# One MoE decoder layer pair on one core: experts ranked by load on the chip, two of the eight turns with two 32-slot tiles

## The reference, cut to what matters

```python
def moe_swiglu(x, w_router, w_gu, w_down):
    b, s, d = x.shape
    xt = x.reshape(b * s, d)                       # 256 tokens x 1024
    logits = (xt @ w_router).astype(jnp.float32)   # 8 experts
    top_vals, top_idx = lax.top_k(logits, TOP_K)   # TOP_K = 2
    gates = jax.nn.softmax(top_vals, axis=-1)
    combine = jnp.sum(jax.nn.one_hot(top_idx, N_EXPERTS, dtype=jnp.float32) * gates[..., None], axis=1)
    y = jnp.zeros((b * s, d), jnp.float32)
    for e in range(N_EXPERTS):
        gu = xt @ w_gu[e]                          # 1024 x 5632, gate and up
        g, u = gu[..., :D_FF_EXPERT], gu[..., D_FF_EXPERT:]
        y = y + combine[:, e:e + 1] * ((jax.nn.silu(g) * u) @ w_down[e])   # 2816 x 1024
    return y.astype(x.dtype).reshape(b, s, d)
```

## Time and profile before

| | us |
|---|---|
| median of 3 runs | 1282.19 (1281.58 to 1284.21) |
| the profiled execution, its own time | 1283.65 |
| its span | 1281.9 |
| TensorE busy | 1226.9 (96%) |
| VectorE / ScalarE busy | 297.0 / 213.8 |
| granted TensorE clock, mean | 0.98 |

### The profile page before, as it was taken

One profiled execution on the slowest core, in us unless ns is written; L12 is line 12 of the kernel. 1 busy time (PEld: TensorE's weight loads), 2 busy tenths in 40 slices (PEclk: granted clock), 3 DMA queues, 4 the chain that ended last, 5 costly groups with the idle time before them and its releaser, 6 DMA issues.

```text
span 1281.9 us, 23541 instructions
## 1 busy us (share of the span) xinstructions
PE 1226.9 (96%) x10557; PEld 656.7 (51%) x10558; DVE 297.0 (23%) x509; ACT 213.8 (17%) x336; POOL 8.1 (1%) x40
## 2 busy tenths in 40 slices
PE   7878999999998889999999999999999999999988
PEld 5548999985884443533533533533533533533433
DVE  4754545533235310001001001001001001001021
ACT  3353443432134100000000000000000000000020
POOL 2000000000000000000000000000000000000000
PEclk9888999999999879999999999999999999999999
DMA  9706655540322346999999999999999999998330
GB/s 333 252 12 216 200 181 184 195 165 33 132 106 92 124 172 251 408 409 405 408 408 384 353 355 375 353 355 371 358 350 375 357 351 373 359 360 331 125 140 33
DMA packets 114170, 344.23 MB, mean 269 GB/s; under 512 B 7773, under 2 KB 30874, under 8 KB 114074
## 3 DMA queue, kind: packets, MB, share of 16 engines
q1 hardware_dynamic: 114074, 342.74, 71.7%
HBM read 341.67 MB, written 1.05 MB: 267 GB/s over the span
## 4 chain that ended last, share of the span: by engine, by line
PE 93%; DVE 4%; ACT 1%; issue 1%; DMA 0%; DVEq 0%; ACTq 0%
PE ps L1624 37%; PE ps L1675 12%; PE ps L1680 6%; PE ps L1385 5%; PE ps L1401 5%; PE ps L1402 5%; PE ps L1403 5%; PE ps L1605 3%; PE ps L1521 2%; PE ps L1774 2%; PE ps L1648 1%; PE ps L1461 1%; PE ps L1693 1%; PE ps L1251 1%; PE ps L1276 1%; PE ps L1298 1%
## 5 line engine op out<-in xcount | busy, mean ns | idle before, releaser
L1624 PE MATMUL ps<-wring,xg 128*32 128x512 f32 (+1 forms) x5376 | 479.6, 503 | 2.8 <-DVE e_h L1152 2.0
L1624 PEld LDWEIGHTS ps<-wring,xg 128*32 128x32 f32 x5376 | 181.1, 110 | 281.7 <-issue 229.5
L1675 PE MATMUL ps<-wring,ehT 128*32 128x512 f32 x1408 | 169.1, 593 | 0.6 <-ACT ehT L737 0.6
L1401 PE MATMUL ps<-dn_high,w_high 128*128 128x256 f32 x352 | 100.6, 286 | 2.5 <-DVE dn_low L1029 2.5
L1402 PE MATMUL ps<-dn_low,w_high 128*128 128x256 f32 x352 | 100.5, 286 | 0.0
L1403 PE MATMUL ps<-dn_high,w_low 128*128 128x256 f32 x352 | 100.4, 285 | 0.0
L1675 PEld LDWEIGHTS ps<-wring,ehT 128*32 128x32 f32 x1408 | 45.2, 110 | 97.4 <-issue 95.9
L1680 PE MATMUL ps<-wring,ehT 128*32 128x512 f32 x704 | 93.2, 592 | 0.0
L1020 DVE TENSOR_TENSOR w_low<-ring,w_high 128x2048 fp32r<-128x2048 f32 x33 | 75.6, 2292 | 58.5 <-ACT w_high L637 58.5
L737 ACT COPY ehT<-ps 128x384 f32<-128x384 f32 x24 | 11.5, 481 | 432.3 <-PE ps L1648 248.8
L1162 DVE COPY ehT<-ps 128x384 f32<-128x384 f32 (+1 forms) x24 | 11.8, 491 | 305.7 <-PE ps L1648 185.6
(11 more groups left out here) (245 smaller groups left out, 962.2 us busy)
## 6 DMA issues: line engine op xcount, KB each, us to landing
wring<-in_w_exp_gu SPq DMA_DIRECT2D x128, 1024.0 KB, 7.7
wring<-in_w_exp_down SPq DMA_DIRECT2D x88, 1024.0 KB, 7.3
wring<-in_w_exp_gu SPq DMA_DIRECT2D x64, 768.0 KB, 8.6
ring<-in_w_ffn_gu SPq DMA_DIRECT2D x44, 512.0 KB, 5.4
ring<-in_w_ffn_down SPq DMA_DIRECT2D x11, 1024.0 KB, 4.9
ring<-in_w_ple_gate SPq DMA_DIRECT2D x4, 1024.0 KB, 4.9
ring<-in_w_q_b SPq DMA_DIRECT2D x4, 1024.0 KB, 4.9
ring<-in_w_o_b SPq DMA_DIRECT2D x4, 1024.0 KB, 6.4
```

Of the source, the lines that this page charges most:

```text
L1401: pe.matmul(out, high_l, high_r, start=first, stop=False)
L1624: return pe.matmul(ps[32 * quarter:32 * quarter + 32, bank, c0:c0 + 2 * nf * P], xg[:, k, 32 * b:32 * b + 32], w[:, :, f * P:(f + nf) * P] ...
L1675: pe.matmul(ps[32 * q:32 * q + 32, 3, :], turned(g, 2 * u + r, b), w[:, r, half * 512:(half + 1) * 512], start=(g == 0 and u == 0 and r == ...
```

## The change

A constant table gives each of the eight turns a number of tiles: turns 3 and 7 have two, the others three. Turn 0 is always expert 0. The other experts are ranked by load on VectorE (`order_experts`), and `TURN_RANK` says which rank comes at which turn: the two smallest loads of experts 1 to 7 come at turns 3 and 7. `expert_at` holds the expert of each turn; SyncE reads it into a register at each turn for the addresses of the loads. Gates and slots are put into the order of the turns (`turn_gate`, `turn_slot`). All steps of an expert take the number of tiles as an argument; for two tiles `gate_up` has 8 (group 2: 12) matmuls in a unit instead of 12 (18), `down` 8 instead of 12, the scatter one part instead of two. The loops of SyncE, ScalarE and VectorE become unrolled. The overflow branch is taken when any turn's load is above its own capacity (96 or 64), and runs two three-tile passes for each such turn. In `first_groups` the transposes of the selection matrix move ahead of group 1. `k_squares` shares its SBUF place with another early tile.

```diff
-NB = SLOTS // 32
+TILES = (3, 3, 3, 2, 3, 3, 3, 2)
+TURN_RANK = (0, 1, 2, 6, 3, 4, 5, 7)
+PINNED = 1024.0
...
     @block.sync
-        loads("body", BODY, 0, lambda i: 1 if BODY[i][0] == "gu" and BODY[i][1] < 2 else 0, "first")
-        with sp_.Fori(1, E - 1) as e:
-            nxt = sp_.snap(e + 1)
-            loads("body", BODY, e, lambda i: nxt if BODY[i][0] == "gu" and BODY[i][1] < 2 else e, "body")
-        loads("alone", ALONE, E - 1, lambda i: E - 1, "end")
-        sp_.wait_ge(route_done, 1)
+        e = 0
+        for n in range(E - 1):
+            if n == 0:
+                sp_.wait_ge(order_done, 1)
+            after = sp_.value_load(expert_at[0:1, n + 1:n + 2], min_val=0, max_val=E - 1)
+            loads("body", BODY, n, lambda i: after if BODY[i][0] == "gu" and BODY[i][1] < 2 else e, "body" if n else "first")
+            e = after
+        loads("alone", ALONE, E - 1, lambda i: e, "end")
...
-        largest = sp_.value_load(counts[0:1, E:E + 1], min_val=0, max_val=T)
-        with sp_.If(largest > SLOTS):
+        largest = sp_.value_load(excess[0:1, E:E + 1], min_val=0, max_val=T)
+        with sp_.If(largest > 0):
...
     @block.gpsimd
         link(pool.tensor_copy(slot_no[:], slot_no_i[:]))
+        link(pool.memset(turn_cap[:], float(SLOTS)))
+        for i in range(E):
+            link(pool.memset(turn_rank[:, i:i + 1], float(TURN_RANK[i])))
+            if i == 0 or TILES[i] < 3:
+                link(pool.memset(turn_cap[:, i:i + 1], 32.0 * TILES[i] + (0.0 if i else PINNED)))
...
     @block.scalar
+        def silu(g, n, kind, nb):
 
             used(kind, "gu", g, n - 1 if kind == "body" and g < 2 else n)
             if g < 2:
-                act.activation(e_silu[:].rearrange("p (b c) n -> p b (c n)", b=NB), ps[:, 0:NB, 0:256], ACT.Silu).then_inc(e_silu_done, 1)
+                act.activation(e_silu[:, 0:2 * nb].rearrange("p (b c) n -> p b (c n)", b=nb), ps[:, 0:nb, 0:256], ACT.Silu).then_inc(e_silu_done, 1)
...
+        def result_high(n, kind, nb):
             used(kind, "down", 2, n)
-            for part in range(2):
-                act.copy(ye_high[:, part, :], ps[:, 3 + part, :]).then_inc(e_y_high, 1)
+            for part in range(nb - 1):
+                act.copy(ye_high[:, part, :], ps[:, 3 + part, :]).then_inc(e_y_high, 4 - nb)
...
     @block.vector
         dve.wait_ge(pos_ready, 1)
-        link(dve.memset(slot_of[:], 0.0))
...
-        dve.tensor_reduce(counts[:, E:], ps[:, 2, 0:E], AX.X, ALU.max)
-        dve.tensor_copy(counts[:, 0:E], ps[:, 2, 0:E]).then_inc(route_done, 1)
+        dve.tensor_copy(load[:], ps[:, 2, 0:E]).then_inc(route_done, 1)
+
+        def order_experts():
+
+            dve.wait_ge(route_done, 1)
+            link(dve.tensor_scalar(load[:, 0:1], load[:, 0:1], PINNED, None, ALU.add))
+            other, own = bc(load[:].unsqueeze(1), [P, E, E]), bc(load[:].unsqueeze(2), [P, E, E])
+            dve.tensor_tensor(cmp_gt[:, 0], other, own, ALU.is_gt)
+            link(dve.tensor_tensor(cmp_eq[:, 0], other, own, ALU.is_equal))
+            link(dve.tensor_tensor(cmp_eq[:, 0], cmp_eq[:, 0], earlier[:], ALU.mult))
+            link(dve.tensor_tensor(cmp_gt[:, 0], cmp_gt[:, 0], cmp_eq[:, 0], ALU.add))
+            link(dve.tensor_reduce(load_rank[:], cmp_gt[:, 0], AX.X, ALU.add))
+            link(dve.tensor_tensor(hot[:], bc(load_rank[:].unsqueeze(1), [P, E, E]), bc(turn_rank[:].unsqueeze(2), [P, E, E]), ALU.is_equal))
+            dve.tensor_tensor(cmp_gt[:, 0], hot[:], bc(slot_no[:, 0, 0:E].unsqueeze(1), [P, E, E]), ALU.mult)
+            link(dve.tensor_tensor(cmp_gt[:, 1], hot[:], bc(load[:].unsqueeze(1), [P, E, E]), ALU.mult))
+            dve.tensor_reduce(turn_no[:], cmp_gt[:, 0], AX.X, ALU.add)
+            link(dve.tensor_reduce(turn_load[:], cmp_gt[:, 1], AX.X, ALU.add))
+            link(dve.tensor_tensor(turn_load[:], turn_load[:], turn_cap[:], ALU.subtract))
+            link(dve.tensor_scalar(turn_load[:], turn_load[:], 0.0, None, ALU.max))
+            dve.tensor_copy(expert_at[:], turn_no[:])
+            dve.tensor_reduce(excess[:, E:], turn_load[:], AX.X, ALU.max)
+            dve.tensor_copy(excess[:, 0:E], turn_load[:]).then_inc(order_done, 1)
+            for src, dst in ((gate, turn_gate), (slot_of, turn_slot)):
+                link(dve.tensor_tensor(hot_of[:], bc(hot[:].unsqueeze(1), [P, NT, E, E]), bc(src[:].unsqueeze(2), [P, NT, E, E]), ALU.mult))
+                link(dve.tensor_reduce(dst[:], hot_of[:], AX.X, ALU.add))
...
+        def picks(slots, base, k, nb):
...
+            c = (nb - 1) * P
             for t in range(NT):
-                ins = dve.tensor_scalar(pick[:, t, :], slot_no[:, base, :], slot_of[:, t, bass.ds(e, 1)], None, ALU.is_equal)
+                ins = dve.tensor_scalar(pick[:, t, 0:c], slot_no[:, base, 0:c], slots(t), None, ALU.is_equal)
             ins.then_inc(e_pick, 1)
...
+        picks(lambda t: slot_of[:, t, 0:1], 0, 0, TILES[0])
+        for half in range(2):
+            gathered(0, half, TILES[0])
+        order_experts()
+        product(0, 0, TILES[0])
+        turned_high(0, 0, TILES[0])
+        turn_picks(1)
+        product(1, 0, TILES[0])
+        for n in range(E - 1):
+            both_experts(n)
...
     @block.tensor
+            m = 32 * nb
             for c in range(4 * half, 4 * half + 4):
                 for t in range(NT):
-                    ins = pe.matmul(ps[:, 7, (c % 4) * SLOTS:(c % 4 + 1) * SLOTS], hs[:, t, c * P:(c + 1) * P], pick[:, t, 64:64 + SLOTS],
+                    ins = pe.matmul(ps[:, 7, (c % 4) * m:(c % 4 + 1) * m], hs[:, t, c * P:(c + 1) * P], pick[:, t, 64:64 + m],
                                     start=(t == 0), stop=(t == NT - 1))
...
                 if g < 2:
-                    for b in range(NB):
+                    for b in range(nb):
                         for j in range(4):
                             ins = part(j, b, 2 * j, 2, b, 0, first)
                 else:
-                    for b in range(NB):
+                    for b in range(nb):
                         for j in range(4):
                             part(j, b, j, 1, b, 0, first)
-                    for b in range(NB):
+                    for b in range(nb):
                         for j in range(2):
                             ins = part((2 * b + j) % 4, b, 4 + j, 1, b // 2, 256, False)
...
-            for i in range(6 if g < 2 else 4):
-                ins = pe.transpose(ps[:, 5 + i // 3, (i % 3) * P:(i % 3 + 1) * P], e_h[:, i, :], ident[:])
-            if g == 2:
+            for i in range(2 * nb if g < 2 else nb + 1):
+                ins = pe.transpose(ps[:, 5 + i // nb, (i % nb) * P:(i % nb + 1) * P], e_h[:, i, :], ident[:])
+            if g == 2 and nb == 3:
...
-                for half in range(2):
+                for half in range(2 if nb == 3 else 0):
                     for r in range(2):
                         q = 2 * half + r
...
             for t in range(NT):
-                for part in range(2):
+                for part in range(nb - 1):
                     for ye in (ye_high, ye_low):
...
-        def first_groups(n, spare=0):
+        def first_groups(n, nb):
 
             for half in range(2):
-                gather(n, half, spare)
-            gate_up("lead", 0, n)
-            gate_up("lead", 1, n, range(0, 4))
-            turn(0, n)
-            turn_pick(n)
-            gate_up("lead", 1, n, range(4, KD))
+                gather(n, half, nb)
+            gate_up("lead", 0, n, nb)
+            turn_pick(n, nb)
+            gate_up("lead", 1, n, nb, range(0, 4))
+            turn(0, n, nb)
+            gate_up("lead", 1, n, nb, range(4, KD))
...
-        first_groups(0)
+        first_groups(0, TILES[0])
         for e in range(E - 1):
             both_experts(e)
-        last_groups(E - 1)
+        last_groups(E - 1, TILES[E - 1])
+        pe.wait_ge(order_done, 1)
```

More of the change, by code:

```diff
@@ new lines, in first_groups, with last_groups @@
+        def first_groups(n, nb):
+            silu(0, n, "lead", nb)
+            turned_low(0, n, nb)
+            pick_turned(n, nb)
+            silu(1, n, "lead", nb)
+        def last_groups(n, nb):
+            turned_low(1, n, nb)
+            silu(2, n, "alone", nb)
+            turned_low(2, n, nb)
+            result_high(n, "alone", nb)
+        def both_experts(n):
+            nb, nb2 = TILES[n], TILES[n + 1]
+            turned_low(1, n, nb)
+            silu(2, n, "body", nb)
+            turned_low(2, n, nb)
+            silu(0, n + 1, "body", nb2)
+            result_high(n, "body", nb)
+            turned_low(0, n + 1, nb2)
+            pick_turned(n + 1, nb2)
+            silu(1, n + 1, "body", nb2)
@@ L1746, in _, with last_groups @@
-        first_groups(0)
+                gather(n, half, nb)
[4 more added lines that the diff above has]
+            gate_up("lead", 1, n, nb, range(4, KD))
+        def last_groups(n, nb):
+            down("alone", 0, n, nb)
```

(27 more changed lines are left out.)

267 lines of the change are left out of this document (119 added, 148 removed).

## The result

| | before | changed |
|---|---|---|
| median, first comparison | 1282.33 us (4 runs) | 1223.78 us (4 runs, 1222.48 to 1224.57) |
| ratio of the two | | 0.954, 95% interval 0.9524 to 0.9557 |
| the same once more (e8) | 1283.71 us (9 runs) | 1223.05 us (5 runs), ratio 0.9532, interval 0.9518 to 0.9546 |
| profiled execution, its span | 1283.65, 1281.9 | 1223.16, 1221.1 |

Faster by 58.5 us in the first comparison and 60.7 in the second. The forecast was 66.0 less, 1216.2 us; the measured 1223.8 lies in the range of 1212.5 to 1226, but above the 1213 to 1222 that the prediction gave for its own case.

The account below looks back on a forecast made before the run. TensorE's matmuls were taken as the bound (busy 96% of the span, DMA 0%). Light turn 32.3, turn 7 33.0 and fixed parts 0.7 sum to 66.0 us saved: 1282.19 to 1216.2 us, range 1212.5 to 1226 (8 in 10).

Parts of the forecast that it names:

- Matmuls of two tiles: Light turn's units: groups 0 and 1 save 13.9 us, group 2 6.9 (by count 5.8), down 9.4.
- Gather: Gather of 64 columns instead of 96 in a light turn: 0 to 0.2 us saved, taken as 0.1.
- Fixed parts: Ahead of the experts: selection transposes moved before group 1 save 0.5 us, memset and reduction off the router path 0.2.
- `order_experts` and the reads: Ranking on VectorE (at most 7 us, covered) and SyncE's seven expert reads (0 to 3 us each): taken as costing nothing.
- rival A: Weight queue falls short in part: at 375 GB/s stalls total 20 us, giving 1236 us; chance 0.08.
- B: Weight queue binds in full at 360 GB/s: light turns save nothing, 1281 us; chance 0.04.
- The arithmetic of the lead: Weights at 407 GB/s: last unit of light turn 3 lands 10 us before use, no stall; heavy turns return 11.4 each.
- the fast stretch: Sign to look for: weight windows show 407 GB/s until about 100 us after turn 3's start, then 360 again.
- rival D: Helper chains bind in turns 3 and 7: 1 us at several places, together up to 5 us, 1221 us; chance 0.09.
- Rival C: A light turn's expert exceeds 64 tokens, so the overflow branch runs two spare passes: 1416 us; chance 0.02.
- what follows the scatter, 2.96 us of TensorE's own sequencer, stays: End of turn 7: TensorE's 2.96 us behind the scatter stays unchanged and still covers the first addition to h.
- the scatter term: Scatter of a light turn, 2.04 us: half its matmuls go, 1.0 us saved.

Follow-up runs that it names:

- e8: Changed kernel unaltered, run once more: 1223.05 us, ratio 0.9532.
- e6: Changed kernel with three light turns, 0 (expert 0, 47 tokens), 4 and 7, instead of 3 and 7: 1194.31 us, ratio 0.9308.
- e1: Changed kernel with three tiles in all eight turns; ranking, register reads and unrolled loops stay: 1282.35 us against 1283.72, ratio 0.9993.
- e5: Changed kernel with the two light turns side by side, turns 6 and 7: 1237.0 us, ratio 0.9635.
- e4: Changed kernel without the overflow branch and the read of its count, on all engines: 1218.31 us, ratio 0.9495.
- e10: As e4, but every engine still reads the largest excess into a register where the branch stood: 1218.71 us, ratio 0.9498.
- e3: Changed kernel with the tail's four gate loads held back until the last addition to h: 1221.59 us, ratio 0.9521.
- e2: Changed kernel with only turn 3 light, turn 7 back at three tiles: 1252.91 us against 1283.72, ratio 0.9763.
- e7: As e6, with the tail's gate loads held back as in e3: 1190.84 us, ratio 0.9278.
- e9: As e3, run beside e8 on the same chip: 1222.02 us, ratio 0.9516.

## Why the prediction was right, and what it missed

The terms, as the traces of the two kernels have them:

| term | forecast | measured |
|---|---|---|
| light turn 3 | 32.3 | 32.0 |
| turn 7 up to its last down unit | 31.4 | 31.2 |
| result chain and last scatter | 1.6 | 1.4 |
| up to the down group 0 of turn 0 | 0.7 | 0.15 |
| from the last scatter to the gate matmuls | 0 | -4.0 |
| sum | 66.0 | 60.8 (spans: 60.8) |

- **Matmuls of two tiles**: right to 1%. A unit of groups 0 and 1 took 1.75 us (forecast 1.74), a down unit 1.72 (1.72). Group 2 took 1.31; by quarters it was 1.30, by the count of matmuls 1.45. The reading of the short windows in the earlier trace rows decided this rightly.
- **Gather**: 2.00 us for 64 columns against 2.02 for 96, so the 0.1 a turn was too optimistic; e6 has eight matmuls of 64 columns in turn 0's gather, one run of them 3.65 us against 3.70 for 96.
- **Turn 7**: 862.19 to the last down unit's end at 1168.31 is 306.1 us, before the same stretch was 337.3 (894.33 to 1231.61).
- **Fixed parts**: the stall ahead of group 1 fell from 2.01 to 1.49 us and the one ahead of the first gather from 1.64 to 1.29, as worked out. But turn 0's down group began at 508.69 in the changed kernel, only 0.15 us earlier than before (508.84): the first `gate_up` took 22.61 us instead of 22.21 and the router's last transposes began 0.36 later. The first of these is the clock: from 460 to 480 us it is granted at 0.85 in the changed kernel and at 0.87 in the one before, 0.4 us of 20. The gain is there and is mostly lost in what this stretch varies by from one execution to the next.
- **`order_experts` and the reads**: right at nothing (e1). The operations ran from 462.0 to 466.9, `order_done` at 465.1, and VectorE was next needed at 485.8.
- **Weights**: right in that no stall came (rival A wrong, B wrong: 403 to 407 GB/s). The arithmetic of the lead was put to the test by e5, where it forecast 8 to 12 us of waits and the trace shows 8.3 as idle time, 13.0 with what goes with them, and by e6 (0 to 7 forecast, 2.7 shown). What I wrote to look for was wrong: the fast stretch lasts 220 us, not 100. The deficit of 21 us at 11.4 a turn needs two turns to be repaid, by my own numbers.
- **Helper steps**: right. No idle time of TensorE between 500 and 1160 us in the changed kernel; rival D wrong. Rival C didn't happen.

The range held by luck in part. Its upper end stood at 1226 to take in rivals D and A, and neither happened; the terms of the forecast itself went up to 1222, and the step that failed brought the time above that.

The step that failed is the sentence that "what follows the scatter, 2.96 us of TensorE's own sequencer, stays". I carried an idle time over without asking what it was made of. Had I asked what a faster last turn brings close to it, part of the answer was in my own weights paragraph: the tail's five loads are 13 us of transfer, and with 31 us less work in the last turn they run on across the branch. In the kernel before the transfers had ended some 4 us ahead of the scatter; in the changed kernel they end 3 us behind it. The later start of the program's transfer is 2.0 of the 2.7 us of idle time. Most of the rest comes from the scatter term: its second half, booked as 1.0 us saved, had covered 0.95 us of the way past the branch. The other 1.25 us are the clock, and they don't go with the idle time: in the traces the first four matmuls of L1520 take 5.2 us in e5, after the longest idle time, 5.4 in e4 after the shortest, and 6.6 and 6.7 in the changed kernel and e8. What sets this stays open. The rest down to the first median's 58.5, some 2 us, is put down to scatter between executions: the second comparison gives 60.7.

The cause, as far as shown: the branch, not the read (e10), not a landing (e3), and longer when weights are in flight. Five traces without them have 2.7 to 3.9 us (before, e2, e3, e7, e9), four with them 5.3 to 6.2 (changed, e5, e6, e8). e1 isn't among them: there the clock fell during the scatter itself and the first addition to h released TensorE. That TensorE waits for the piece of program is still an inference, since no record names the wait; for it speak that the piece comes in every trace with the branch and in neither without, and that TensorE goes on 2.65 to 3.1 us behind its start in ten traces, whatever the start. It also fits a rule of the Trainium skill, page "Runtime: NRT & Kernel Launch", section "Instruction fetch mechanics": a taken branch whose target isn't held already makes the engine fetch it by DMA before it goes on. The page gives no time for it. That passing an unused body is a taken branch for TensorE is an inference too. Why the transfer begins later beside weights, no run here shows.

## What to carry to other kernels

When a stage gets shorter, look at every idle time behind it that no other engine ends: here the way past a branch left an engine idle for 3 to 4 us in quiet and 5 to 6 while weights streamed, and the transfers that used to end before it may now run across it. Look also at what such an idle time overlaps: work that it partly hides behind is not saved in full when it goes. Where matmuls are packed in quarters, the time of a unit is that of the quarter with most work, so dropping a tile can save more than its share. A queue with a lead can pay for a stage that is faster than the transfers, if the stages after it repay the lead before the next one; put such stages apart.

## What the runs showed of the hardware that I had not expected

- Passing an overflow branch that isn't taken: 4.3 to 4.7 us of TensorE's time behind the scatter when 400 GB/s flow beside it (idle 5.67 and 5.3 against 1.01 and 1.00 without the branch), and some 5 us on SyncE's queue.
- The instruction queue's 16 KB piece at that place starts 2.0 to 2.1 us after the scatter's first matmul with no weights in flight and 3.7 to 4.6 with them; TensorE goes on 2.65 to 3.1 us after its start either way.
- A register read from SBUF under the same traffic costs nothing visible, neither on TensorE (e10) nor seven times on SyncE (e1).
- The granted clock falls to the lower level behind the last scatter in every kernel, also in e4 and e10 with 1.0 us of idle time there (the result chain's 1.6 us stand ahead of it); in e1 it fell already during the scatter (0.61 in the window from 1236 to 1238 us). The four matmuls that follow vary from 5.2 to 6.7 us with it, not in the order of the idle times.
- The same code ahead of the experts takes 441.4 to 443.7 us from one execution to the next, as much as most of the spread between runs of one kernel (1.2 to 3.8 us, 5.9 in e1).
